# Keys' projection between the index score products, and the top-k of two more tiles inside the mixers

## The reference, cut to what matters

```python
c_q, k_a, v_a, k_i, w_i, q_b, z_f, i_b, g_b = split(h @ w_in)
q_a, q_i = rms_norm(c_q) @ w_uq, rms_norm(c_q) @ w_uq_idx    # 8 heads of 64; 16 index heads of 64
score = sum_h w_i[h] * relu(q_i[h] . layer_norm(k_i))        # causal
idx = top_k(score, 256)                                      # the attention sees only these keys
o_a = attention over the selected keys, with ALiBi
o_b = gated linear recurrence (HGRN2) of q_b, z_f, i_b, gated by silu(g_b)
h = LN(alpha * h + concat(o_a, o_b) @ w_out)
```

## Time and profile before

| what | us |
|---|---|
| median of 3 runs (2773.99 to 2776.44) | 2776.26 |
| the profiled execution | 2778.51 |
| its span, first to last instruction | 2776.8 |
| TensorE busy in the span | 2614.8 |
| VectorE busy | 1294.2 |
| GpSimd busy | 1067.2 |
| ScalarE busy | 844.2 |

### The profile page before, as it was taken

One profiled execution on the slowest core, in us unless ns is written; L12 is line 12 of the kernel. 1 busy time (PEld: TensorE's weight loads), 2 busy tenths in 40 slices (PEclk: granted clock), 3 DMA queues, 4 the chain that ended last, 5 costly groups with the idle time before them and its releaser, 6 DMA issues.

```text
span 2776.8 us, 36408 instructions
## 1 busy us (share of the span) xinstructions
PE 2614.8 (94%) x14303; PEld 2219.0 (80%) x14303; DVE 1294.2 (47%) x2469; ACT 844.2 (30%) x1385; POOL 1067.2 (38%) x636
## 2 busy tenths in 40 slices
PE   6778999779999997899999999999999999999996
PEld 5767999767888876788998777888878788888885
DVE  3889999766666541333333322332323232233224
ACT  2574222122433322322222323232332232233221
POOL 1222111364544431544333433444433344445443
PEclk8899999869999998999999989999999999999998
DMA  2001122123333214323322323223322233333331
GB/s 97 20 12 46 34 93 74 57 80 110 104 99 95 93 58 155 109 63 92 107 86 83 91 61 91 70 82 109 101 79 69 84 91 107 91 91 99 115 111 48
DMA packets 276468, 232.93 MB, mean 84 GB/s; under 512 B 10448, under 2 KB 257296, under 8 KB 276304
## 3 DMA queue, kind: packets, MB, share of 16 engines
q1 hardware_dynamic: 268112, 222.13, 26.8%
q10 hardware_dynamic: 8192, 8.52, 0.9%
HBM read 217.91 MB, written 12.71 MB: 83 GB/s over the span
## 4 chain that ended last, share of the span: by engine, by line
PE 56%; DMA 1%; POOL 1%; ACT 1%; DVE 1%; issue 0%; POOLq 0%; SPq 0%; ACTq 0%; DVEq 0%
PE banks L1785 33%; PE banks L1801 19%; PE banks L1818 1%; PE banks L1823 1%; PE banks L1835 1%; DMA draw<-in_w_down 1%; POOL dL L1711 1%; DMA raw<-in_w_up 1%; POOL wL L1704 0%; PE banks L1509 0%; ACT dH L1885 0%; ACT wH L1879 0%; DVE y L1487 0%; DVE y L1985 0%; PE banks L1820 0%
## 5 line engine op out<-in xcount | busy, mean ns | idle before, releaser
L1785 PE MATMUL banks<-hL,wH 128*128 128x512 f32 (+1 forms) x1760 | 620.4, 353 | 16.3 <-ACT hid L1894 14.1
L1704 POOL TENSOR_TENSOR wL<-raw,wH 128x2048 fp32r<-128x2048 f32 x88 | 406.3, 4617 | 595.3 <-ACT wH L1879 595.3
L1785 PE MATMUL banks<-hH,wL 128*128 128x512 f32 (+1 forms) x1760 | 619.4, 352 | 0.0
L1785 PE MATMUL banks<-hH,wH 128*128 128x512 f32 (+1 forms) x1760 | 617.2, 351 | 0.0
L1965 DVE TENSOR_TENSOR hid<-hid,banks 128x512 f32<-128x512 f32 (+1 forms) x110 | 64.4, 585 | 760.6 <-PE banks L1785 648.8
L1785 PEld LDWEIGHTS banks<-hL,wH 128*128 128x128 f32 x1760 | 332.8, 189 | 65.5 <-ACT hid L1894 15.2
L1785 PEld LDWEIGHTS banks<-hH,wL 128*128 128x128 f32 x1760 | 332.7, 189 | 46.3
L1785 PEld LDWEIGHTS banks<-hH,wH 128*128 128x128 f32 x1760 | 333.2, 189 | 45.0
L1711 POOL TENSOR_TENSOR dL<-draw,dH 128x1024 fp32r<-128x1024 f32 x88 | 220.8, 2509 | 375.0 <-ACT dH L1885 375.0
L1985 DVE TENSOR_TENSOR y<-y,banks 128x512 f32<-128x512 f32 (+1 forms) x340 | 233.1, 686 | 219.0 <-PE banks L1801 217.9
L1801 PE MATMUL banks<-dH,hidL 128*128 128x512 f32 (+1 forms) x748 | 303.9, 406 | 2.3 <-issue 2.3
(11 more groups left out here) (228 smaller groups left out, 4303.3 us busy)
## 6 DMA issues: line engine op xcount, KB each, us to landing
raw<-in_w_gate SPq DMA_DIRECT2D x88, 512.0 KB, 4.7
raw<-in_w_up SPq DMA_DIRECT2D x88, 512.0 KB, 6.0
draw<-in_w_down SPq DMA_DIRECT2D x88, 512.0 KB, 3.5
w_out_part<-in_w_out SPq DMA_DIRECT2D x64, 512.0 KB, 4.1
slab<-in_w_in SPq DMA_DIRECT2D x10, 1024.0 KB, 5.7
va<-in_x SPq DMA_DIRECT2D x8, 512.0 KB, 4.9
vg_scratch<-y ACTq DMA_DIRECT2D x32, 128.0 KB, 1.7
y<-in_x SPq DMA_DIRECT2D x8, 512.0 KB, 7.5
```

What stands on the lines that cost most here:

```text
L1704: nc.gpsimd.tensor_tensor(wL[:, ff % 2, :, :, :].rearrange("p g k f -> p (g k f)"), raw[:, :, :, :].rearrange("p g k f -> p (g k f)"), wH[ ...
L1785: last = nc.tensor.matmul(banks[:, GU + (2 * q + g) % 3, 0:n], wt[:, ff % 2, g, k, :], h[:, k, a:a + n], start=(k == 0 and part == 0), sto ...
```

## The change

In `projection`:

- The loop that writes `order` has only `cq`, `x`, `idx`, `stats` and `norm`, for T from 0 to 10, with the splits of slabs 0 and 1 at T = 9. The score products no longer stand between them.
- After it come the index queries of tile 2 and then all 208 score units one by one. Between them stand the index queries of the next tile (after the fourth and the seventh unit of a tile), and the 96 k steps of the twelve blocks of slabs 0 and 1 (`FILL`), spread evenly over the units, each with its copy out of the bank. When slab 0's last block is out, slab 2 is split, and so on.
- After the last score unit the other ten slabs follow; the values are now the last two.
- x's transposes use three pairs of banks in turn instead of one; the keys' blocks use banks 2 and 3.
- `w_qi` lies in `y`; the distances are made by GpSimd after the last index query, and tiles 0 and 1 get theirs by an iota of their own. The raw slabs lie in `va`'s memory up to the last two, so that they can be loaded early.
- `EARLY` is tiles 2 to 5.

In `mixers`, the late top-k covers tiles 6, 7 and 8, each with its own `top8` and semaphore. Tile t's 32 rounds are spread over steps 1 to 8t - 4, its mask is made at the end of step 8t - 3, and GpSimd places it in step 8t - 2.

```diff
+LATE_TILES = (NT - 3, NT - 2, NT - 1)
...
     SLABS = [(col + SW * half, fm, dest, half) for col, fm, dest in (
-        (COL_KA, True, "ka"), (COL_VA, False, "va"), (COL_ZF, True, 1), (COL_QB, True, 0), (COL_IB, False, 0),
-        (COL_GB, False, 1)) for half in range(512 // SW)]
+        (COL_KA, True, "ka"), (COL_ZF, True, 1), (COL_QB, True, 0), (COL_IB, False, 0), (COL_GB, False, 1),
+        (COL_VA, False, "va")) for half in range(512 // SW)]
...
-    EARLY = TM[:-1]
+    EARLY = [m for m in TM if m not in LATE_TILES]
...
-    for T in range(NT + 3):
-        if T == NT + 2:
-            order += [("split", 0), ("split", 1)]
-        take("cq", T - 2)
-        take("sc", T - 3, FIRST_TOPK, 0)
-        take("x", T)
-        take("sc", T - 3, FIRST_TOPK, 1)
-        take("idx", T - 1)
-        take("sc", T - 3, FIRST_TOPK, 2)
-        take("stats", T - 1)
-        take("qi", T - 2, FIRST_TOPK, 0)
-        take("norm", T - 1)
-        take("sc", T - 3, FIRST_TOPK, 3)
-        take("qi", T - 2, FIRST_TOPK, 1)
-        take("sc", T - 3, FIRST_TOPK, 4)
+    for T in range(NT + 2):
+        take("cq", T - 2)
+        take("x", T)
+        take("idx", T - 1)
+        take("stats", T - 1)
+        take("norm", T - 1)
+        if T == NT:
+            order += [("split", 0), ("split", 1)]
+    order += [("qi", TM[0], 0), ("qi", TM[0], 1)]
+
+    def slab_part(n):
+        u, k = divmod(n, DC)
+        order.append(("slab", u, k))
+        if k == DC - 1:
+            order.append(("out", u))
+            j = slab_units[u][0]
+            if u == last_unit[j] and j + 2 < len(SLABS):
+                order.append(("split", j + 2))
+
+    FILL = FILL_UNITS * DC
+    for i, (m, _, _, _) in enumerate(units):
+        order.append(("sc", i))
+        at = [n for n, u in enumerate(units) if u[0] == m].index(i)
+        if m + 1 < NT and at in (3, 6):
+            order.append(("qi", m + 1, at // 3 - 1))
+        if i == last_of_tile[m]:
+            order.append(("causal", m))
+        for n in range(i * FILL // len(units), (i + 1) * FILL // len(units)):
+            slab_part(n)
+    order.append(("scored", 0))
+    for n in range(FILL, len(slab_units) * DC):
+        slab_part(n)
...
     def split(j):                                  # GpSimd
             if j >= 2:
                 pool.wait_ge(slab_psum, last_unit[j - 2] + 1)
             else:
-                pool.wait_ge(qi_psum, 2 * NQ)
+                pool.wait_ge(idx_psum, NT)
...
-    LATE0, LATE1 = 1, NU - A_HEADS - 3
-    late_rounds = {i: [r for r in range(ROUNDS) if LATE0 + r * (LATE1 - LATE0) // ROUNDS == i] for i in range(NU)}
+    LATE0 = 1
+    LATE1 = {t: t * A_HEADS - 3 for t in LATE_TILES}
+    late = {t: scores_at(score, t, 0, NKEYS[t]) for t in LATE_TILES}
+    late_rounds = {i: [(t, r) for t in LATE_TILES for r in range(ROUNDS)
+                       if LATE0 + r * (LATE1[t] - LATE0) // ROUNDS == i] for i in range(NU)}
...
-            for r in late_rounds.get(i, ()):
+            for t, r in late_rounds.get(i, ()):
                 if r:
-                    dve.wait_ge(taken, 2 * r)
-                nc.vector.max(top8[:, :], late).then_inc(taken, 1)
+                    dve.wait_ge(taken[t], 2 * r)
+                nc.vector.max(top8[t][:, :], late[t]).then_inc(taken[t], 1)
```

More of the change, by code:

```diff
@@ L244, in units_of @@
-    def units_of(m, part):
-        mine = [i for i, u in enumerate(units) if u[0] == m]
-        return mine[len(mine) * part // PARTS:len(mine) * (part + 1) // PARTS]
+            order.append((what, m))
+    for T in range(NT + 2):
[5 more added lines that the diff above has]
+        if T == NT:
+            order += [("split", 0), ("split", 1)]
+    order += [("qi", TM[0], 0), ("qi", TM[0], 1)]
[7 more added lines that the diff above has]
+                order.append(("split", j + 2))
@@ L332, in _ @@
                     pool.wait_ge(qi_lo, 2 * nqi + b + 1)
-            elif what == "sc" and part[0] == PARTS - 1:
+            elif what == "causal":
                 pool.wait_ge(acc_done, last_of_tile[m] + 1)
@@ L338, in _ @@
                 split(m)
-        for j in range(2, len(SLABS)):
-            split(j)
+                splits += 1
+        pool.wait_ge(qi_psum, 2 * NQ)
+        nc.gpsimd.iota(dist.bitcast(I32), pattern=[[1, L]], base=1 - L, channel_multiplier=0).then_inc(dist_done, 1)
+        pool.wait_ge(dist_done, 2 * FIRST_TOPK + 1)
+        nc.gpsimd.tensor_copy(dist, dist.bitcast(I32)).then_inc(dist_done, 1)
+        pool.wait_ge(dist_done, 2 * FIRST_TOPK + 2)
         for i, m in enumerate(EARLY):
@@ L402, in _ @@
             if what == "sc":
[L403 to L411, removed]
@@ L412, in _ @@
-        pe.wait_ge(relu_done, len(units))
-        for i, (j, fm, dest, idx, a, n) in enumerate(slab_units):
-            pe.wait_ge(slab_lo, j + 1)
-            if i >= 8:
-                pe.wait_ge(slab_out, i - 7)
-            H, Lo = slabH[j % 2], slabL[j % 2]
-            for k in range(DC):
-                for part, (h, w) in enumerate(((hL, H), (hH, Lo), (hH, H))):
-                    first, stop = k == 0 and part == 0, k == DC - 1 and part == 2
+                i = m
+                tile, h, k0, kn = units[i]
@@ new lines, in _ @@
+                pe.wait_ge(qi_lo, 4 * nth_q[tile] + 4)
+                if i >= SB:
+                    pe.wait_ge(relu_done, i - SB + 1)
+                nc.tensor.matmul(banks[:, score_bank(i), 0:kn], qiT[:, tile % 2, h, :], kiL[:, k0:k0 + kn],
+                                 start=True, stop=False)
+                nc.tensor.matmul(banks[:, score_bank(i), 0:kn], qiT[:, tile % 2, h, :], kiH[:, k0:k0 + kn],
+                                 start=False, stop=True).then_inc(sc_psum, 1)
+            if what == "scored":
+                pe.wait_ge(relu_done, len(units))
+                pe.wait_ge(qi_done, 2 * NQ)
@@ new lines, in _ @@
+            if what == "slab":
+                i, k = m, part[0]
+                j, fm, dest, idx, a, n = slab_units[i]
+                H, Lo, bank = slabH[j % 2], slabL[j % 2], slab_bank[i]
+                if k == 0:
+                    pe.wait_ge(slab_lo, j + 1)
+                    if i == 0:
+                        pe.wait_ge(idx_dve, NT)
+                        pe.wait_ge(cqT_done, NT)
+                    if used_before[i] is not None:
+                        pe.wait_ge(slab_out, used_before[i] + 1)
+                for p, (h, w) in enumerate(((hL, H), (hH, Lo), (hH, H))):
+                    first, stop = k == 0 and p == 0, k == DC - 1 and p == 2
@@ L441, in _ @@
                 split(m)
-                continue
-            t0, n = TILES[m]
+            if what == "out":
+                out_of_bank(m)
+            t0, n = TILES[m] if m < NT else (None, None)
             if what == "x":
@@ L511, in _ @@
+                i, kn = m, units[m][3]
+                act.wait_ge(sc_psum, i + 1)
+                if i >= NR:
+                    act.wait_ge(acc_done, i - NR + 1)
+                nc.scalar.activation(relu[:, i % NR, 0:kn], banks[:, score_bank(i), 0:kn], ACT.Relu)\
+                  .then_inc(relu_done, 1)
+            if what == "scored":
+                act.wait_ge(acc_done, len(units))
         for s in range(NS):
-            act.wait_ge(stored[s], 16 * ((staged - s + NS - 1) // NS))
+            act.wait_ge(stored[s], 16 * ((staged[0] - s + NS - 1) // NS))
```

194 lines of the change are left out of this document (94 added, 100 removed).

## The result

| kernel | median of its runs, us | ratio to before (95% interval) |
|---|---|---|
| before | 2776.35 (2773.99 to 2778.25) | |
| after | 2823.31 (2820.78 to 2827.09) | 1.0167 (1.0155 to 1.018) |

A forecast was written before the change was run, and what follows sets the result against it. The prediction took TensorE to bound the late projection and the mixers, with VectorE becoming the bound in the mixers' steps 0 to 31. Projection -31 and mixers +37 gave +6 on 2776.3: 2782.3 us, 8 in 10 between 2756 and 2809.

The forecast's parts named there:

- Parts 1 to 3: Prologue, score products with keys between, ten slabs: mixers start at 507 instead of 538.2, -31 us (bounds -45 and -15).
- The score stage: Projection, first to last score product: TensorE 136 us, VectorE 132, overlapping imperfectly to 143 us (136 to 155).
- slab 2's split: GpSimd work amid tile 6's score products: might stop VectorE's accumulations, 0 to +4.6 us, 4.6 taken.
- Part 4: Mixers: the late top-k rounds of tiles 6 and 7 make VectorE the bound, +37 us (bounds +21 and +55).
- The bill: Mixers' cost of the added rounds: +33 us in tiles 0 to 3, +4 in tiles 4 and 5, sum +37.
- The clock: Rival, mixers: TensorE's waits lower its clock, +10 us on the forecast, perhaps +16 to +22 with later steps; chance 0.12.
- Its condition: Sign for the clock rival in the mixers: TensorE's clock in tiles 2 and 3 under 0.9.
- the waits left: Mixers, steps 0 to 31: 14 us of VectorE's 65 us of waits would stay unfilled by rounds.
- the sums fit: Mixers, tiles 4 and 5: 35.4 us of rounds against 22 and 20 us of VectorE idle, costing only +4.
- VectorE busy over 90% in steps 1 to 31: Sign that the forecast is right, in the mixers, together with 210 us for those steps in place of 177.
- the bound test of the forecast: Mixers, steps 0 to 31: VectorE's 196.4 us of work exceed 177.3, so VectorE bounds, at least 19 us over.
- The waits take the rounds: Rival, mixers: VectorE's waits in steps 0 to 31 fill nearly whole, bill 21 to 24 us, total 2767; chance 0.31.

The follow-up runs named there:

- warm_fit: After plus unused 256-column TensorE products: three at h = 1, five at h = 3 (tiles 2, 4, 5), eight at h = 5; 2787.05 us, ratio 1.0039.
- odd2: After with only tiles 7 and 8 late, their rounds in odd steps alone, in front of the output quarter's sum; 2758.77 us, ratio 0.9933.
- even2: After with only tiles 7 and 8 late, their rounds in even steps alone, in front of `on` at h = 4; 2821.72 us, ratio 1.0167.
- warm: After plus eight unused 512-column TensorE products in front of the wait for `on` at h = 5, tiles 1 to 5; 2828.88 us, ratio 1.0184.

## Why the prediction was wrong

**Parts 1 to 3, the projection: right.** 114.7 for 117, 263.8 for 260, 508.8 for 505, the top-k at 422 for 417, the start at 510.5 for 507: -27.7 for -31. The score stage took 149 us for 143, inside its bounds, with both engines under full (141.1 and 129.5 of 149.3). For VectorE I had 132, or 127 if slab 2's split left the accumulations alone. It does not leave them alone. While GpSimd splits slab 2, one accumulation lasts as long as the split, 4.94 us, where the one before it took 0.63:

```profile
198.96 4.98 POOL L340 TENSOR_TENSOR shared<-va,shared 128x2048 fp32r<-128x2048 f32 x1
...
198.87 0.63 DVE L623 SCALAR_TENSOR_TENSOR y<-y,wi 128x392 f32<-128x392 f32 x1 [1.12 <-ACT y L539]
...
199.42 4.94 DVE L623 SCALAR_TENSOR_TENSOR y<-y,wi 128x392 f32<-128x392 f32 x1
```

The Trainium skill (SBUF — State Buffer, "Who interferes with whom") has a VectorE instruction with two SBUF inputs contend with GpSimd's reads. The trace agrees: 4.3 us lost (4.94 less 0.63), where the forecast took 4.6.

**Part 4, the direction: right, and the step that failed is its bill.** A round cost what it was priced at: from start to start a MAX8 took 0.89 us at 784 keys (744.40 to 745.29) and 1.02 at 912 (750.59 to 751.61). VectorE's column in tiles 0 to 3 came to 190.2 us where the forecast had 196.4. In part that is a change outside the sum: the six multiplications of `on` there took 9.0 us before and 4.1 in after, while nine of `key_arg` and `lnw` went from 7.9 to 10.3; the rest isn't accounted for. Three of the six, before and then after:

```profile
L1400 DVE TENSOR_TENSOR on<-on,rsh 128x512 f32<-128x512 f32 x3 | 4.7, 1569 | 0.0
```
```profile
L1434 DVE TENSOR_TENSOR on<-on,rsh 128x512 f32<-128x512 f32 x3 | 2.0, 678 | 0.0
```

The bill was +37, with +55 as its upper bound, and it came to +74. The forecast asked how many of VectorE's waits the rounds would fill, and let TensorE run at its clock of before once it had its inputs. The clock was a rival at 0.12, priced at +10 on top for tiles 1 to 3, perhaps +16 to +22 with later steps, half of its loss thought hidden beside VectorE. By warm_fit it is 36 us, and it lies in tiles 1 to 5: tile 4, at 1.00 before, has 0.82. A third of the time at half clock, as the rival had it, is a mean clock of 0.83, and tiles 1 to 3 had 0.69, 0.87 and 0.82. Their gain in warm_fit is 4.5 + 6.5 + 8.7 = 20 us, which is the rival's 20 before it took half away as hidden; tiles 4 and 5 give 12.4 + 5.1 more. The loss isn't hidden, because the half clock falls on the very quarters that VectorE waits for (5.95 and 6.53 us in tile 4). Its condition, under 0.9 in tiles 2 and 3, is met (0.87 and 0.82), so this rival is what happened in half of the excess, at 1.6 times its highest price (22) and 3.6 times its lowest (10).

**The rest isn't the forecast's sum either.** At full clock warm_fit still has +36.5, the size of the +37, but in other places: +23.4 in tiles 0 to 3 (+33 forecast) and +14.1 in tiles 4 and 5 (+4 forecast). In the first, 6 of the 10 us are VectorE's shorter column, and the waits left are 10 us (200.7 less 190.5) for 14. In the second "the sums fit" was the error: tile 4's VectorE has 52.9 us of work in 63.1, and still waits for quarters. That agreement of the totals is partly chance. Missing from the sum were also TensorE's waits at h = 1 and h = 3, of 1.2 to 2.5 us each in after: I had followed only `on` at h = 5.

**The sentence "VectorE busy over 90% in steps 1 to 31" fails**, and so do its 210 us for tiles 0 to 3 (220.4). VectorE was busy 40.53 of 42.7 and 44.14 of 48.8 in tiles 0 and 1, 52.80 of 63.5 and 52.73 of 65.4 in tiles 2 and 3, 83 and 81%. By the bound test of the forecast (two columns, the longer one sets the time) after cannot be explained: both columns fit and the time is longer than either. *The waits take the rounds* falls for after, but it is what odd2 does with one tile less: mixers +6 for 32 more rounds.

**The state of the clock.** The Trainium skill (TensorE: Matmul & The Clock Gate, "What's actually happening") says that the throttled state is the default and that activity releases it. The rows agree in direction: half clock begins in or shortly behind TensorE's waits and ends during work. In tile 4, 2.19 us of waiting were followed by 13.7 us at half with TensorE busy throughout, which cost about 7 us (an estimate: half of 13.7). Not every wait does it: in tile 5 one of 1.24 us at 824.39 was followed by full clock up to 847, and odd2, whose TensorE waits 1.3 to 1.7 us for `on` in each of tiles 2 to 5, kept 0.99 there. What decides between them no run here isolates.

## What to carry to other kernels

Putting work into an idle engine's queue costs what it delays, not what it lasts: look up which of the engine's results another one waits for, and place the work behind them and in front of the wait that it is to fill (odd2 against even2, the same rounds, 63 us). Where TensorE already works close to full, a new wait of 2 us may have to be priced with half clock after it, on the products that the waiting engine needs. And move only as much as the other stage needs: tile 6's rounds bought 1.2 us, while VectorE's top-k ended 87 us before the last slab product (421.9 and 508.8).

## What the runs showed of the hardware beyond that

- In after's tile 4, waits of TensorE of 2.19, 2.49 and 5.29 us went with 13.7, about 3 and about 10 us at half clock, so the length of the wait doesn't give that of the half clock. In warm the same 2.19 us of waiting was followed by 17 us.
- Products that nobody uses, fitted into the waits, made the program faster by 36 us (2823.31 to 2787.05). With twice the columns they gave 6.
- A filler of 512 columns in fp32 took 0.88 us, one of 256 0.44.
- One fp32 accumulation on VectorE stood for the whole of a GpSimd split: 4.94 us in place of 0.63. The multiplications of `on` took 1.57 us each in before and 0.68 in after; what GpSimd did beside them wasn't looked at.
- GpSimd's mask of 128 columns (line 323) took 0.29 us at 133.04, 165.99 and 188.46, 1.95 at 216.35, and 8.23 at 241.49, where VectorE had 18 accumulations in a row, 8.98 us together. It was no cost here, as nothing waited for it. That the accumulations held it is argued from the overlap alone and wasn't tried.
